# A transformer block's mixer, reordered: projection tiles between index scores, rotations and attention units

## The reference, cut to what matters

```
h = rmsnorm(x) * (1 + sc1) + sh1
x = x + g1 * mixer(h)
h = rmsnorm(x) * (1 + sc2) + sh2
x = x + g2 * (silu(h @ Wg) * (h @ Wu)) @ Wd
```

## Time and profile before

| | us |
|---|---|
| three runs | 3840.33, 3889.02, 3896.49 |
| median | 3889.02 |
| the profiled execution: its own time | 3870.83 |
| its span, first to last instruction | 3869.3 |
| mean granted TensorE clock, 1 = 2.4 GHz | 0.954 |

### The profile page before, as it was taken

One profiled execution on the slowest core, in us unless ns is written; L12 is line 12 of the kernel. 1 busy time (PEld: TensorE's weight loads), 2 busy tenths in 40 slices (PEclk: granted clock), 3 DMA queues, 4 the chain that ended last, 5 costly groups with the idle time before them and its releaser, 6 DMA issues.

```text
span 3869.3 us, 43856 instructions
## 1 busy us (share of the span) xinstructions
PE 3646.4 (94%) x18028; PEld 2810.9 (73%) x18028; DVE 1290.6 (33%) x2255; ACT 791.6 (20%) x1631; POOL 1601.3 (41%) x1020
## 2 busy tenths in 40 slices
PE   5999999999999999999999979989999998989998
PEld 3656677788876566677777857777888887767886
DVE  4832121321146412112311166554112135553113
ACT  2232231110012322311100033432011012331011
POOL 1312536656553125166455533123333343234664
PEclk9989899999999998699999989999999999999999
DMA  6243212333331433023444221012333321113231
GB/s 205 68 129 114 84 41 88 109 97 96 98 98 58 149 103 95 6 92 103 131 131 142 87 76 44 23 44 89 98 109 127 108 70 58 33 46 126 91 97 66
DMA packets 409615, 351.08 MB, mean 91 GB/s; under 512 B 9797, under 2 KB 406853, under 8 KB 409418
## 3 DMA queue, kind: packets, MB, share of 16 engines
q1 hardware_dynamic: 401568, 340.82, 28.4%
q10 hardware_dynamic: 7850, 7.47, 0.6%
HBM read 346.16 MB, written 2.10 MB: 90 GB/s over the span
## 4 chain that ended last, share of the span: by engine, by line
PE 88%; DVE 7%; ACT 3%; issue 1%; DMA 1%; POOL 0%; ACTq 0%; DVEq 0%; POOLq 0%
PE psum L467 24%; PE psum L469 24%; PE psum L468 24%; PE psum L675 3%; PE psum L442 3%; PE psum L664 2%; PE psum L811 1%; PE psum L782 1%; PE psum L454 1%; DVE psum L1590 1%; PE psum L577 1%; PE psum L648 1%; PE psum L650 1%; DVE k L2048 1%; DMA raw_weights<-in_ada_w 1%
## 5 line engine op out<-in xcount | busy, mean ns | idle before, releaser
L417 POOL TENSOR_SCALAR weights_hi<-raw_weights 128x1024 fp32r<-128x1024 f32 (+3 forms) x508 | 503.4, 991 | 2196.8 <-PE psum L469 1742.1
L467 PE MATMUL psum<-h_hi,weights_hi 128*128 128x512 f32 (+1 forms) x2896 | 1125.7, 389 | 63.7 <-DVE h_lo L1614 53.1
L420 POOL TENSOR_TENSOR weights_lo<-raw_weights,weights_hi 128x1024 fp32r<-128x1024 f32 (+3 forms) x508 | 1107.1, 2179 | 42.4
L468 PE MATMUL psum<-h_lo,weights_hi 128*128 128x512 f32 (+1 forms) x2896 | 1101.3, 380 | 0.0
L469 PE MATMUL psum<-h_hi,weights_lo 128*128 128x512 f32 (+1 forms) x2896 | 1101.2, 380 | 0.0
L467 PEld LDWEIGHTS psum<-h_hi,weights_hi 128*128 128x128 f32 x2896 | 550.1, 190 | 197.4 <-issue 80.8
L469 PEld LDWEIGHTS psum<-h_hi,weights_lo 128*128 128x128 f32 x2896 | 549.5, 190 | 112.1
L468 PEld LDWEIGHTS psum<-h_lo,weights_hi 128*128 128x128 f32 x2896 | 550.5, 190 | 108.2 <-issue 3.6
L467 PE MATMUL psum<-hidden_hi,weights_hi 128*128 128x512 f32 (+1 forms) x1120 | 411.9, 368 | 0.0
L468 PE MATMUL psum<-hidden_lo,weights_hi 128*128 128x512 f32 (+1 forms) x1120 | 411.6, 367 | 0.0
L469 PE MATMUL psum<-hidden_hi,weights_lo 128*128 128x512 f32 (+1 forms) x1120 | 411.2, 367 | 0.0
(11 more groups left out here) (242 smaller groups left out, 3665.5 us busy)
## 6 DMA issues: line engine op xcount, KB each, us to landing
raw_weights<-in_ada_w SPq DMA_DIRECT2D x96, 1024.0 KB, 5.3
raw_weights<-in_w_mlp SPq DMA_DIRECT2D x64, 1024.0 KB, 5.4
raw_weights<-in_w_in SPq DMA_DIRECT2D x56, 1024.0 KB, 5.3
raw_weights<-in_w_ffn_in SPq DMA_DIRECT2D x88, 512.0 KB, 5.2
raw_weights<-in_w_in SPq DMA_DIRECT2D x34, 512.0 KB, 4.0
raw_weights<-in_w_out SPq DMA_DIRECT2D x16, 1024.0 KB, 5.0
raw_weights<-in_w_ffn_out SPq DMA_DIRECT2D x16, 1024.0 KB, 5.0
raw_weights<-in_w_branch SPq DMA_DIRECT2D x56, 128.0 KB, 2.3
```

The lines of the kernel that those rows point to most:

```text
L417: gpsimd.tensor_scalar(whi[:, r, c0:c1], raw[:, raw_slot, c0:c1], 1.0, 1.0, ALU.mult, ALU.mult).then_inc(*split_hi.up(*key, half))
L420: gpsimd.tensor_tensor(wlo[:, r, c0:c1], raw[:, raw_slot, c0:c1], whi[:, r, c0:c1].bitcast(F32), ALU.subtract).then_inc(*split.up(*key, half))
L467: tensor.matmul(out, sh, mh, start=first, stop=False, skip_group_check=shared)
L468: tensor.matmul(out, sh, ml, start=False, stop=False, skip_group_check=shared)
```

## The change

`project` is gone. Its tiles are issued step by step (one step is three matmuls) by a generator `tile1`, in four stages, with banks of their own. Per stage, `FILL` lists the tiles:

```diff
+FILL = {"index": [("A", "q", c) for c in range(3)],
+        "top": ([("A", which, c) for which in "vk" for c in range(3)] + [("B", which, c) for which in "vq" for c in range(3)]),
+        "A": [("B", "k", c) for c in range(3)],
+        "B": ([("C", "v", c) for c in range(3)] + [("C", "f", 0)] + [("C", "q", c) for c in range(3)]
+              + [("C", "k", 0), ("C", "fcol", 0), ("C", "k", 1), ("C", "k", 2)]),
+        "C": [("gate", "", g) for g in range(6)]}
+FILL_BANKS = {"index": (7, 5, 6), "top": (0, 1, 2, 3), "A": (4, 5), "B": (4, 5), "C": (4, 5)}
+ROPE_ORDER = (0, 3, 1, 4, 2, 5)
```

```diff
+            fill = pace(fill1(l, kind), fill_steps(kind), len(units) + 2)
             scores(0)
             for u in range(len(units) + 2):
                 if u == 2:
                     tensor.wait_ge(*moved.at(l, kind, "vt", 2))
                 if u + 1 < len(units):
                     scores(u + 1)
+                next(fill)
                 if 1 <= u <= len(units):
                     turn(u - 1)
```

**Index stage.** The two queries' rotations come after the key's tile, and tiles stand between:

```diff
+            swap_query(0, 0)
+            swap_query(1, 1)
+            w = split_slab((l, "qi", 1))
+            linear((l, "qi", 2), w, 0, (hh, hl), [(0, T)], [3])
...
+            linear((l, "qi", 3), w, P, (hh, hl), [(0, T)], [2])
...
+            swap_query(2, 3)
+            fill = fill1(l, "index")
+            for k in range(KT):
+                next(fill)
+                if k == 2:
+                    swap_query(3, 2)
             tensor.wait_ge(*roped.at(l, "ki"))
-            tensor.wait_ge(*roped.at(l, "qi", 3))
+            weave = pace(fill, 2 * KT, HI * (TT - 1))
```

**Top.** A new stage after the scores, twelve tiles; the six rotations of A lie inside B's q tiles, and the four "rope" modulation slabs come after the third tile and on:

```diff
+        def top(l):
+            steps = ada_steps("rope", l)
+            turns = iter(ROPE_ORDER)
+            for n, (kind, which, c, bk) in enumerate(fill_banks("top")):
+                for k, _ in enumerate(tile1(l, kind, which, c, bk)):
+                    if (kind, which) == ("B", "q") and k in (1, 5):
+                        t = next(turns)
+                        swap(qk[:, t, :], T, 4 + t // 3, (l, "A", t), perm, moved.at(l, "A", "qk"[t // 3], t % 3))
+                if n >= 2:
+                    next(steps, None)
+            finish(steps)
```

**Branches.** The gate tiles of the first pair are done in attention C, copied with their bias and given the sigmoid afterwards in place:

```diff
-                for br in range(3):
+                for br in range(3 if jj else 0):
                     w = split_slab((l, "gate", jj, br))
...
-                if jj == 0:
-                    for kind, n in (("A", 2), ("B", 2), ("C", 2)):
-                        tensor.wait_ge(*o_lo.at(l, kind, n))
                 for br in range(3):
+                    if jj == 0:
+                        tensor.wait_ge(*o_lo.at(l, KINDS[br], 2))
```

**Slab order** follows, with modulation slabs between:

```diff
+        matrix((l, "qi", 0), wi, OQI, 256)
+        matrix((l, "ki"), wi, OKI, P)
         ada(("norm1", l))
-        matrix((l, "ki"), wi, OKI, P)
...
+        matrix((l, "qi", 1), wi, OQI + 256, 256)
+        part("A", "q", 0)
+        part("A", "q", 1)
+        part("A", "v", 0)
+        part("A", "v", 1)
+        ada_some("rope", 0, 1)
+        part("A", "k", 0)
+        ada_some("rope", 1, 3)
+        part("A", "k", 1)
+        ada_some("rope", 3, 4)
+        for which in "vq":
+            part("B", which, 0)
+            part("B", which, 1)
+        part("B", "k", 0)
+        ada_some("A", 0, 4)
+        part("B", "k", 1)
+        ada_some("A", 4, 8)
+        part("C", "v", 0)
+        part("C", "v", 1)
+        ada_some("B", 0, 2)
+        part("C", "q", 0)
+        ada_some("B", 2, 4)
+        part("C", "q", 1)
+        part("C", "k", 0)
+        ada_some("B", 4, 6)
+        part("C", "k", 1)
+        ada_some("B", 6, 8)
```

**Space.** B's q and k go into the end of the output buffers that C fills later, B's values and four of the six first gates into columns 0 to 255 of `X`. So the context tokens are loaded there only in the last layer, before the feed stage:

```diff
-        scalar.dma_start(X[:, :, 0:TC], a["ctx_t"].rearrange("(k p) t -> p k t", p=P)).then_inc(*loaded["ctx"].up())
...
+            else:
+                scalar.dma_start(X[:, :, 0:TC], a["ctx_t"].rearrange("(k p) t -> p k t", p=P)).then_inc(*loaded["ctx"].up())
```

B's first bias diagonals are fetched at the start of attention A:

```diff
-            if kind == "B":
-                scalar.wait_ge(*moved.at(l, "B", "k", 2))
+            fill = pace(fill1(l, kind), fill_steps(kind), len(units) + 2)
+            if kind == "A":
                 diagonals(l, 0)
```

More of the change, by code:

```diff
@@ L152, in steps2, with fill_steps, fill_banks, fill_key @@
     return sum(STEPS2[kind] + (0 if last or kind not in "qu" else 4) for kind, m in TILES2[head])
+def fill_steps(stage):
+    return sum(1 if which == "fcol" else KT for _, which, _ in FILL[stage])
+def fill_banks(stage):
+    n = 0
+    for item in FILL[stage]:
+        yield *item, FILL_BANKS[stage][n % len(FILL_BANKS[stage])]
+        n += 1
+def fill_key(l, kind, which, c):
+    return (l, "gate", 0, c // 2, c % 2) if kind == "gate" else (l, "f") if which == "f" else (l, kind, which, c)
 def pace(steps, total, slots):
@@ L539, in index, with fill1 @@
+        def fill1(l, stage):
+            for kind, which, c, bk in fill_banks(stage):
+                if which == "fcol":
+                    forget_columns(l, bk)
+                    yield
+                else:
+                    yield from tile1(l, kind, which, c, bk)
         def index(l):
@@ new lines, in forget_log, with fill1 @@
+        def forget_log(l):
+            scalar.wait_ge(*dve_misc.at(l, "absf"))
+            scalar.activation(F, F, ACT.Exp, scale=-1.0).then_inc(*act_misc.up(l, "expf"))
+            scalar.wait_ge(*act_misc.at(l, "expf"))
+            scalar.activation(F, F, ACT.Ln, bias=1.0).then_inc(*act_misc.up(l, "lnf"))
+        def fill1(l, stage):
+            for kind, which, c, bk in fill_banks(stage):
+                for k in range(1 if which == "fcol" else KT):
+                    if k == 3 and late:
+                        move_values1(l, *late.pop())
+                    if k == 4 and kind == "C" and FORGET_AT.get((which, c)) == "log":
+                        forget_log(l)
+                    if k == KT - 1:
+                        move_tile1(l, kind, which, c, bk)
+                    yield
@@ L1158, in project, with top @@
+        def top(l):
+            steps = ada_steps("rope", l)
+            fill = fill1(l, "top")
+            for n in range(len(FILL["top"])):
+                for k in range(KT):
+                    next(fill)
+                if n >= 2:
                     next(steps, None)
-                finish(steps)
+            finish(steps)
         def attend(l, kind):
@@ L1733, in select, with top, forget @@
             vector.memset(maska[0:CHUNK, 0, CHUNK:P], NEG).then_inc(*masked.up(l))
[L1735 to L1742 removed]
+        def top(l):
+            select(l)
+            for t in ROPE_ORDER:
+                rope(qk[:, t, :], 4 + t // 3, (l, "A", t), moved.at(l, "A", "qk"[t // 3], t % 3))
+            ada_finish("rope", l)
+        def forget(l, part, bk):
+            if part == "absolute":
                 vector.wait_ge(*moved.at(l, "f"))
```

388 lines of the change are left out of this document (206 added, 182 removed).

## The result

| us | before | changed |
|---|---|---|
| median | 3875.32 (3840.33 to 3896.49, 4 runs) | 3759.95 (3758.74 to 3764.6, 4 runs) |
| ratio, 95% interval | | 0.9713, 0.9633 to 0.9793 |
| the profiled execution | 3870.83 | 3759.26 |
| its span | 3869.3 | 3757.9 |

The forecast was 3759, so time and direction came out. It was a saving of 111.6 us from the profiled execution; between the medians it is 115.4. Its terms did not all come out: the clock was better by some 10 us a layer, and work and seams together were more by about as much. The profile shows that first.

A forecast was written before the change was run, and what follows sets the result against it. The prediction took TensorE, busy 94% of the span, as the bound. Mixer savings of 46.6 and 62.0 us, with the start 111.6 us, took the profiled 3870.8 us to 3759, range 3703 to 3845.

The forecast's parts named there:

- New mixer: Per layer, first projection to last attention unit without gate tiles: (372 + 8 + 10) / 0.965 = 404.1 us.
- Clock: Largest term: woven mixers get 0.965, as the second block's woven attention does, instead of 0.87, the mean of both layers.
- rival of an unchanged clock: Mixers: pieces come and waits go, but the clock stays at 0.87; 448 us per layer, 3847 us in all; chance 0.13.
- W = 372: TensorE's work per layer's mixer in us, after taking off idle time and clock loss; layers gave 373 and 370.
- Seams: Breaks in rows of products on TensorE: some 90 per layer at 0.09 us each, 8 us per layer.
- Idle time: TensorE's waits in a mixer: 10 us per layer left, from 28.0 and 26.2; modulation waits stay at 3.7.
- Cover: Attention stages: a piece between scores and transposes hides the transposes' waits; longer normalisations, possibly 23 us per layer, counted as nothing.
- VectorE's slack: Index stage and top: selection ends near 191, rotations near 204, TensorE at 222; 18 us to spare, no cost.
- ScalarE, VectorE and tables: Attention B's added copies, logarithm with table loads, and scan: neither engine becomes late, costed at nothing.
- Start: Kernel's start: moving the 1 MB context load to the last layer's feed stage makes it 3.0 us earlier.
- Slabs late: Mixers: half of 48 weight slabs come late at 8.7 us each, 209 us, giving 3968 us; chance 0.04.
- Everything covered: Mixers: idle 4 us, clock near 1.0, no seams; 376 us per layer, 3703 us in all; chance 0.08.

The follow-up runs named there:

- e6: The changed kernel with attention C's 48 pieces (gate tiles) all put behind C's last unit: 3821.46 us.
- e3: The changed kernel with attention A's 24 pieces all put behind A's last unit: 3788.86 us.
- e4: The changed kernel with each piece cut in two on TensorE, its first product ahead of the next unit's scores: 3781.83 us.
- e2: The changed kernel with ScalarE's copy of a modulation row moved ahead of the exponential, and in top ahead of a tile's copy: 3758.05 us.
- e7: The changed kernel with each turn's piece behind the transposes instead of ahead of them, on TensorE alone: 3777.43 us.
- e9: The changed kernel with earlier modulation copies, A's pieces from its first turn, and four of C's pieces ahead of C's first scores: 3739.47 us.
- e12: The kernel of e3 run again for another profile, a single run: 3782.64 us.

## Why the prediction was right, and what was wrong in it

**Total and sign.** 3759 against 3759.95. New mixer 404.1 against 405.5 and 405.8, alike in both layers: shown.

**Clock, mis-sized.** The step took 0.965 from the second block's attention, a loss of 14 us per layer; the windows show 0.99, 4 us. That pieces raise the clock is shown by e6 and by e3 with its two further profiles. The rival of an unchanged clock fell. So did its support in the Trainium skill (TensorE: Matmul & The Clock Gate, "A second HAM failure mode: psum-queue depth-cycling"), as far as it was applied here: transposes and outputs rotate over one bank instead of two, and the granted clock is 1.00, 1.00 and 0.98 in attention A, B and C.

**Work, mis-sized.** W = 372 rests on the step "a TensorE at half rate does half of its work", and 373 and 370 in layers of different clocks were read as support. Their difference was the warning. e6 has both clocks with the same instructions; windows of its mixers:

```profile
65.90:537.20 471.30, 459.13 (x2149) 307.03 (x2149) 188.42 (x497) 134.32 (x323) 134.40 (x94) 0.91 0.28 87
1131.70:1581.80 450.10, 434.66 (x2149) 293.01 (x2149) 187.48 (x497) 134.36 (x323) 134.28 (x94) 0.97 0.30 93
```

By the same split they give 471.3 - 12.2 - 42.4 = 416.7 and 450.1 - 15.4 - 13.5 = 421.2: 4.5 us less work where 28.9 us more are lost to the clock, as 3 in 20 in the earlier trace rows. The windows give the clock to two digits, which is 2 us of such a mixer, so both are rough. The windows of e6's bare C have a smaller error: 77.30 - 0.48 x 77.9 = 39.9 and 51.78 - 0.15 x 55.5 = 43.5, which is 3.6 in 29. So not all of TensorE's time doubles at half clock, and the split understates the work by 0.12 to 0.15 us per us of loss. Corrected so, the mixer before holds 372 + (0.12 to 0.15) x 49.6 = 378 to 379 us of work, 6 to 7 more than W.

**Seams, too low.** The changed kernel's mixer has 439.1 - 11.5 - 4.4 = 423.2; corrected likewise and without the gate tiles that is 423.2 + 0.6 - 33.6 = 390. So 11 to 12 us are left for seams, where 8 were taken. The number of breaks was nearly right, 90 against 111 - 15 = 96 in the trace. The price of 0.09 came from the front side alone: e4's 0.17 to 0.19 would make 16 to 18 us of these 96. The two ways differ by 4 to 7 us, and how much of the mixer is work and how much seams stays open by so much; that both together are 10 us more than forecast doesn't depend on it.

So per layer: 404.1 + 10 (work and seams) + 1.5 (idle) - 10 (clock) = 405.6. The errors hid each other, and the closeness of the total is partly luck.

**Idle time.** 11.5 us against 10, but otherwise made: the stall of B's first v slab was 0.4 and not 1.5, A's and B's starts 1.2 each (B's was taken to be gone), and the modulation waits didn't stay at 3.7 but rose to 7.8 (3.4 in top, 2.3 in A, 2.1 in B). The step that they "stay, since the piece stands ahead of the transposes" failed. It overlooked that ScalarE's copy stands behind its probabilities' copy, which waits for transposes that now come later in TensorE's turn, and that top has the same order of copies. e2 shows that the place of the copy is the cause.

**Cover.** The piece ahead of the transposes covers them: shown by e7 (8.7 us back). The 23 us per layer that longer normalisations beside GpSimd's splits might have cost didn't come: the 64 normalisations of layer 0 take 500 ns each instead of 447, and the transposes wait 0.4 us. The index gaps vanished as said, shown by the waits alone.

**VectorE's slack.** 18 us were expected between rotations that are ready and their use. VectorE does finish the selection at 192.3, but each rotation can only follow its swap, and the last swap stands at the end of top: the last rotation ends at 227.9, after A's first scores have begun. The slack is before the rotations (13.9 us), not behind them; the claim that it costs nothing held.

**ScalarE, VectorE and tables.** Costed at nothing; attention B shows only the waits told above (2.5 us for modulation rows, 1.2 for its first maximum), C none. **Start.** 3.0 us for the load is shown (3.2); the 3 us more that came with the new slab order were missed. **Slabs late** fell: 0.4 us in a mixer. **Everything covered**, 3703 us, needed seams at nothing and W = 372; even e9, with 3.2 us idle per mixer and a clock of 0.99, takes 3739.

## What to carry to other kernels

On an engine that is busy 94% of the time, read the granted clock by stage before the waits: here stretches of small matmuls that were 99% busy ran at half clock, and a few large matmuls between them were worth more than all the waits that they covered. Price each break in a row of large matmuls at both of its sides (0.17 to 0.19 us here, of which the front side showed 0.11), and count the breaks in the trace. When an edit removes waits and the time stays, look for a dip that took the place, and fill the stretch ahead of it.

## What the runs showed of the hardware that was not expected

The clock of 1.2 GHz isn't tied to idle time: bare C ran at 0.52 with 0.6 us idle in 77.9 (e6), and at 0.85 with 3.7 idle in the other layer. The same instructions kept 1.00 or dipped for 27 us from run to run (e3, e12), and at A's start, with turn 0 the same on TensorE, e2 dipped for 17 us, one profile of the changed kernel for some 3 and the other not at all.

VectorE's three operations that write the selection's mask took 1220 ns each in the changed kernel, beside GpSimd's splits of the weights, and 354 ns before, without them. That the splits are the cause wasn't tried alone. VectorE's rows of before, then of the changed kernel:

```profile
L1729 DVE TENSOR_SCALAR select_mask<-softmax_buffers 128x256 bf16<-128x256 f32 (+2 forms) x3 | 0.9, 354 | 0.0
```

```profile
L1872 DVE TENSOR_SCALAR select_mask<-softmax_buffers 128x256 bf16<-128x256 f32 (+2 forms) x3 | 3.5, 1220 | 0.0
```

It cost nothing here, because VectorE waits for the swaps anyway. Where VectorE is the bound, moving GpSimd's work beside it would be a change of its own.
